# First blocks of an expert loop: overflow tables by counting, the residual's stores ahead of a gather, gates turned after unit 9, down biases in other PSUM banks

## The reference

```python
logits = hf @ w_router + b_router              # 32 experts, top 4 of each token
gates = softmax(top_vals)
# assignments sorted by expert, each expert padded to blocks of 128 rows
gu = xb @ w_gate_up[e] + b_gate_up[e]          # per block of 128 rows
gate, up = min(gu[:, :D], 7), clip(gu[:, D:], -7, 7)
act = (up + 1) * (gate * sigmoid(1.702 * gate))
y = act @ w_down[e] + b_down[e]
out = x2 + sum over the four experts of gate * y
```

## Time and profile before

| | before |
|---|---|
| median of 3 runs | 1726.53 us (1725.62 to 1729.35) |
| the profiled execution | 1726.46 us |
| its span, first to last instruction | 1724.6 us |
| PE busy | 1657.2 us (96% of the span) |
| DVE busy | 1351.2 us (78%) |
| ACT busy | 1094.6 us (63%) |
| POOL busy | 323.4 us (19%) |
| mean granted TensorE clock | 0.982 |
| bytes moved | 482.34 MB, mean 280 GB/s |

### The profile page before, as it was taken

The page is one execution under the profiler, slowest core; times in us unless marked ns, Lnnn a source line. Parts: engine busy times, 40 slices in busy tenths (PEclk is TensorE's granted clock), DMA queues, the critical chain, the costliest instruction groups (busy, mean ns, idle before and its releaser), DMA issues.

```text
span 1724.6 us, 23842 instructions
## 1 busy us (share of the span) xinstructions
PE 1657.2 (96%) x7974; PEld 1352.2 (78%) x7974; DVE 1351.2 (78%) x1089; ACT 1094.6 (63%) x989; POOL 323.4 (19%) x178
## 2 busy tenths in 40 slices
PE   7999999999987979999999999999999999999995
PEld 5797777888975758888888888888888888888884
DVE  4864555633546969999999999999999999999994
ACT  5323434322343657778777787778877788777873
POOL 0000000600004742122211321122211221112210
PEclk9999999999996989999999999999999999999998
DMA  8231222332535799999999999999999999999993
GB/s 269 74 97 51 73 74 74 92 122 74 180 146 186 266 322 364 377 364 376 381 385 372 361 381 382 380 373 365 382 379 377 373 365 388 380 373 364 377 387 82
DMA packets 211683, 482.34 MB, mean 280 GB/s; under 512 B 12539, under 2 KB 55075, under 8 KB 195123
## 3 DMA queue, kind: packets, MB, share of 16 engines
q1 hardware_dynamic: 201024, 453.99, 70.1%
q0 software_dynamic: 10624, 27.87, 7.9%
HBM read 469.05 MB, written 21.67 MB: 285 GB/s over the span
## 4 chain that ended last, share of the span: by engine, by line
PE 89%; POOL 3%; DVE 2%; issue 2%; DMA 2%; ACT 1%; SPq 0%; ACTq 0%; POOLq 0%; DVEq 0%
PE ps L575 27%; PE ps L577 27%; PE ps L576 27%; PE ps L755 2%; PE ps L761 2%; PE ps L779 2%; POOL slot_records L1487 1%; PE ps L689 1%; PE ps L678 1%; DMA out<-r 1%; PE ps L650 1%; DMA r<-in_x 1%; PE ps L669 0%; POOL work L1506 0%; PE ps L722 0%
## 5 line engine op out<-in xcount | busy, mean ns | idle before, releaser
L1236 DVE TENSOR_TENSOR zT<-raw,zT 128x2048 fp32r<-128x2048 f32 x96 | 221.4, 2307 | 70.4 <-ACT zT L988 67.1
L1236 DVE TENSOR_TENSOR w_lo<-more_raw,w_hi 128x2048 fp32r<-128x2048 f32 x96 | 218.0, 2298 | 15.9 <-ACT w_hi L988 15.8
L1236 DVE TENSOR_TENSOR zT<-more_raw,zT 128x2048 fp32r<-128x2048 f32 x96 | 220.0, 2291 | 4.0 <-ACT zT L988 4.0
L1236 DVE TENSOR_TENSOR w_lo<-raw,w_hi 128x2048 fp32r<-128x2048 f32 x96 | 217.3, 2290 | 0.0
L575 PE MATMUL ps<-w_hi,xT 128*128 128x512 f32 x512 | 216.3, 422 | 0.0
L575 PE MATMUL ps<-zT,xT 128*128 128x512 f32 x512 | 204.7, 400 | 10.9 <-DVE zT L1236 10.9
L988 ACT ACTIVATE zT<-more_raw 128x2048 fp32r<-128x2048 f32 x96 | 183.4, 1911 | 33.9 <-PE ps L577 33.9
L576 PE MATMUL ps<-zT,xT 128*128 128x512 f32 x512 | 201.2, 393 | 0.0
L577 PE MATMUL ps<-zT,xT 128*128 128x512 f32 x512 | 201.1, 393 | 0.0
L577 PE MATMUL ps<-w_hi,xT 128*128 128x512 f32 x512 | 201.0, 393 | 0.0
L576 PE MATMUL ps<-w_lo,xT 128*128 128x512 f32 x512 | 200.9, 392 | 0.0
(11 more groups left out here) (244 smaller groups left out, 3358.7 us busy)
## 6 DMA issues: line engine op xcount, KB each, us to landing
more_raw<-in_w_gate_up SPq DMA_DIRECT2D x129, 1024.0 KB, 6.0
raw<-in_w_gate_up SPq DMA_DIRECT2D x127, 1024.0 KB
raw<-in_w_down SPq DMA_DIRECT2D x65, 1024.0 KB
more_raw<-in_w_down SPq DMA_DIRECT2D x63, 1024.0 KB, 6.7
raw<-in_w_in SPq DMA_DIRECT2D x29, 1024.0 KB, 5.2
r<-in_x SPq DMA_DIRECT2D x8, 512.0 KB, 7.1
raw<-in_w_branch_conv SPq DMA_DIRECT2D x4, 1024.0 KB, 4.7
raw<-in_w_out SPq DMA_DIRECT2D x4, 1024.0 KB, 4.7
```

What stands on the lines that cost most here:

```text
L1236: nc.vector.tensor_tensor(expert_pair(1, c), chunk, expert_pair(0, c).bitcast(F32), ALU.subtract).then_inc(split_lo, 2)
```

## The change

- `over_experts` no longer makes two comparisons, a product and a product with the expert's number. It compares the overflow block's number with the running end `inc32` of each expert once, and sums the outcome: the count of experts that end before the block. One instruction on 15 columns adds 1 and caps at 32. The selectors and the block numbers follow in the same function.
- POOL's five stores of `x2` move ahead of `gather_next(1)` and of the tables.
- On PE, the gates' transpose moves from after unit 3 to after unit 9, `down_bias(0)` from after unit 7 to after unit 13, `down_bias(1)` from after unit 11 to after the turn of block 1's rows, and PE waits for the last addition before block 1. Both write banks 0, 1, 4 and 5 in place of 4 to 7, so `down_bias(0)` also waits for the first activation.
- On DVE, the split of chunk 3 moves ahead of `place_records`, the gates by expert to after split 4, copy and first activation to after split 6, the additions (now two instructions each) to after split 0 of block 1 and after the second activation, and split 1 of block 1 to the end.
- ACT waits for the additions at the head of each iteration.

```diff
--- before.py
+++ after.py
@@ -305,7 +305,6 @@
         byexp = work[:, 0:512].rearrange("p (b k e) -> p b k e", b=NB, k=TOPK)
         byoff = work[:, 512:1024].rearrange("p (b k e) -> p b k e", b=NB, k=TOPK)
         ov1 = work[:, 3072:3072 + MAXOVER * NE].rearrange("p (j e) -> p j e", e=NE)
-        ov2 = work[:, 3584:3584 + MAXOVER * NE].rearrange("p (j e) -> p j e", e=NE)
         xTh, xTl = xT[:, 0:KD], xT[:, KD:2 * KD]
         aT = oT[:, :, :, :].rearrange("p a b (c n) -> p (a b c) n", n=P)
         aTh, aTl = aT[:, 0:KD], aT[:, KD:2 * KD]
@@ -806,25 +805,25 @@
             def down_bias(n):
 
                 for b in range(NB):
-                    last = pe.matmul(ps[:, bk_D + b, :], gT[NE * b:NE * b + NE, :],
+                    last = pe.matmul(ps[:, bk_A + 4 * (b // 2) + b % 2, :], gT[NE * b:NE * b + NE, :],
                                      bdn[NE * b:NE * b + NE, 512 * n:512 * n + 512], start=True, stop=True)
                 last.then_inc(down_bias_pe, 1)
 
             for j in range(16):
                 gate_up(0, j)
-                if j == 3:
+                if j == 9:
                     pe.wait_ge(gates_ok, 1)
                     pe.transpose(ps[:, bk_D, 0:P], gmat.rearrange("p b e -> p (b e)"), ident).then_inc(gT_pe, 1)
-                if j == 7:
+                if j == 13:
                     pe.wait_ge(gT_ok, 1)
                     pe.wait_ge(down_bias_in, 16 * NB)
+                    pe.wait_ge(act_ok, 2)
                     down_bias(0)
-                if j == 11:
-                    pe.wait_ge(x2_biased, 1)
-                    down_bias(1)
-            pe.wait_ge(x2_biased, 2)
             next_rows(0, 0)
             next_rows(0, 1)
+            pe.wait_ge(x2_biased, 2)
+            down_bias(1)
+            pe.wait_ge(x2_biased, 4)
             with pe.Fori(1, nblk) as g:
                 pe.wait_ge(turned_read, tile(g, BEGIN))
                 for j in range(16):
@@ -1047,6 +1046,7 @@
             turned(0, ROWS1, xTh[:, 4:8, :], bk_T + 1)
             sigmoid(0, 1)
             with sc.Fori(1, nblk) as g:
+                sc.wait_ge(x2_biased, 4)
                 store_y(g, unit_base(g), g)
                 for c in range(2, CPE):
                     split_expert(g, c)
@@ -1359,6 +1359,7 @@
                                         xTh[:, 4 * half:4 * half + 4, :].bitcast(F32),
                                         ALU.subtract).then_inc(turned_read, 1)
             split_expert(0, 2)
+            split_expert(0, 3)
             place_records()
             gates()
             ve.wait_ge(blocks_ok, 2)
@@ -1392,28 +1393,27 @@
 
                 ve.wait_ge(down_bias_pe, n + 1)
                 cols = slice(512 * n, 512 * n + 512)
-                nc.vector.tensor_tensor(x2[:, :, cols], x2[:, :, cols], ps[:, bk_D:bk_D + NB, :],
-                                        ALU.add).then_inc(x2_biased, 1)
-
-            for c in range(3, 8):
+                for pair, bank in ((slice(0, 2), bk_A), (slice(2, 4), bk_D)):
+                    nc.vector.tensor_tensor(x2[:, pair, cols], x2[:, pair, cols], ps[:, bank:bank + 2, :],
+                                            ALU.add).then_inc(x2_biased, 1)
+
+            for c in range(4, 8):
                 split_expert(0, c)
-                if c == 3:
+                if c == 4:
                     gates_by_expert()
-                if c == 4:
+                if c == 6:
                     ve.wait_ge(gT_pe, 1)
                     nc.vector.tensor_copy(gT, ps[:, bk_D, 0:P]).then_inc(gT_ok, 1)
-                if c == 6:
-                    add_down_bias(0)
-                if c == 7:
                     clamp_up(0, 0)
                     activate(0, 0)
-                    add_down_bias(1)
             split_expert(1, 0)
-            split_expert(1, 1)
+            add_down_bias(0)
             turned(0, ROWS0, xTh[:, 0:4, :], xTl[:, 0:4, :], bk_T)
             turned(0, ROWS1, xTh[:, 4:8, :], xTl[:, 4:8, :], bk_T + 1)
             clamp_up(0, 1)
             activate(0, 1)
+            add_down_bias(1)
+            split_expert(1, 1)
             with ve.Fori(1, nblk) as g:
                 for c in range(2, CPE):
                     split_expert(g, c)
@@ -1493,8 +1493,6 @@
 
 
             jrow = cst[:, C_IOTA:C_IOTA + MAXOVER].unsqueeze(2).to_broadcast([P, MAXOVER, NE])
-            erow = cst[:, C_IOTA:C_IOTA + NE].unsqueeze(1).to_broadcast([P, MAXOVER, NE])
-            off_b = off32.unsqueeze(1).to_broadcast([P, MAXOVER, NE])
             inc_b = inc32.unsqueeze(1).to_broadcast([P, MAXOVER, NE])
             over = slice(NE, MAXBLK)
 
@@ -1508,22 +1506,15 @@
 
             def over_experts():
 
-                link(nc.gpsimd.tensor_tensor(ov1, jrow, off_b, ALU.subtract))
+                link(nc.gpsimd.tensor_tensor(ov1, jrow, inc_b, ALU.subtract))
                 link(nc.gpsimd.tensor_scalar(ov1, ov1, 0.5, None, ALU.is_gt))
-                link(nc.gpsimd.tensor_tensor(ov2, jrow, inc_b, ALU.subtract))
-                link(nc.gpsimd.tensor_scalar(ov2, ov2, 0.5, None, ALU.is_lt))
-                link(nc.gpsimd.tensor_tensor(ov1, ov1, ov2, ALU.mult))
-                link(nc.gpsimd.tensor_tensor(ov2, ov1, erow, ALU.mult))
+                link(nc.gpsimd.memset(eb[:, MAXBLK:NCOL], 1.0))
                 link(nc.gpsimd.tensor_copy(eb[:, 0:NE], cst[:, C_IOTA:C_IOTA + NE]))
-                link(nc.gpsimd.memset(eb[:, MAXBLK:NCOL], 1.0))
-                total(eb[:, over], ov2)
-
-            def over_selectors():
-
+                total(eb[:, over], ov1)
+                link(nc.gpsimd.tensor_scalar(eb[:, over], eb[:, over], 1.0, float(NE), ALU.add, ALU.min))
                 link(nc.gpsimd.tensor_scalar(sel[:, over, :], eb[0:3 * NE, over].unsqueeze(2).to_broadcast(
                     [3 * NE, MAXOVER, P]), cst[0:3 * NE, C_RMOD:C_RMOD + 1], None, ALU.is_equal))
-                link(nc.gpsimd.tensor_scalar(eb, eb, 1.0, -1.0, ALU.max, ALU.add))
-                nc.gpsimd.tensor_copy(ublk[:, 0:NCOL], eb).then_inc(over_ok, 1)
+                nc.gpsimd.tensor_scalar(ublk[:, 0:NCOL], eb, -1.0, None, ALU.add).then_inc(over_ok, 1)
                 gp.wait_ge(over_ok, 1)
 
             gp.wait_ge(blocks_ok, 2)
@@ -1555,14 +1546,13 @@
                 gp.wait_ge(y_out, 16 * blocks)
                 gp.sem_inc(rows_free, 1)
 
+            gp.wait_ge(x2_biased, 4)
+            for b in range(NB):
+                gp.dma_start(out_v[:, b, :], x2[:, b, :]).then_inc(out_set, 16)
+            gp.dma_start(out[S:S + P, :], x2[:, 0, :]).then_inc(out_set, 16)
             gp.wait_ge(slots_in, 16)
             gather_next(1)
             over_experts()
-            gp.wait_ge(x2_biased, 2)
-            for b in range(NB):
-                gp.dma_start(out_v[:, b, :], x2[:, b, :]).then_inc(out_set, 16)
-            gp.dma_start(out[S:S + P, :], x2[:, 0, :]).then_inc(out_set, 16)
-            over_selectors()
             gp.wait_ge(out_set, 16 * (NB + 1))
             with gp.Fori(1, but_one) as before:
                 g = before + 1
```

## The result

The changed kernel takes 1713.99 us in the median of 4 runs (1712.57 to 1715.58), the kernel before 1726.39 us (1725.62 to 1729.35; one run more than in the table of before). The ratio is 0.9925 with a 95% interval of 0.9908 to 0.9942: faster by 0.6 to 0.9%. The forecast was 1713.5. The profiled execution took 1712.57 us, with a span of 1710.7 against 1724.6, 13.9 us less.

The account below looks back on a forecast made before the run. PE is the bound, and POOL's chain decides when block 2 may go on. Gains of 4.1 - 0.3 + 13.3 - 5.2 + 1.0 = 12.9 us from 1726.46 us give 1713.5, range 1707.5 to 1720.5.

Parts of the forecast that it names:

- Block 0: Start of the kernel: PE resumes for block 1 at 568.5 instead of 572.64, 4.1 us earlier, with 0.3 charged for clock.
- POOL's chain: Records to uix copy, ahead of block 2: copy at 604.6, so block 2's whole 13.33 us excess goes.
- The 3.6 us in hand: Before block 2: margin between the uix copy at 604.6 and ACT wanting it at 608.2.
- What is late next is PE's own pace: Block 2: with the uix copy in time, PE's own work sets the time; block 2 takes about 35.6 us.
- 0.3 + 5.2 - 1.0: Block 1: 0.3 us restart clock, 5.2 lost to selectors holding DVE, 1.0 gained as four instructions that held DVE go.
- The gather ... cost 0: Block 2's rows, queued behind 2.62 MB of stores, land about 596, wanted at 598.3: cost 0, bounds 0 and 6 us.
- rival (B): POOL's queue is late after all, gather lands about 601, 3 us more wait with clock behind: about 1718; chance 0.2.
- The selectors: Block 1, about 597.5: selectors hold DVE 5.0 us, 1.5 covered, 3.5 PE wait plus 1.7 half clock: 5.2 us lost.
- (A): Selectors meet DVE's idle or PSUM work in block 1, so no loss: 1709.4; chance 0.2.
- (C): Stores and weights bunch on the DMA engines from 579 to 593, splits wait: 1720 to 1723; chance 0.08.
- (D): POOL's queue gets only what weights leave, gather lands at 634, 36 us late: slower, 1747; chance 0.05.
- (E): Some 8 of the tables' 11.4 us were waiting for DVE and stay; copy at 612, 4 us stall: about 1718; chance 0.05.

Follow-up runs that it names:

- POOL's part alone: Kernel before plus tables by counting, stores ahead of the gather and selectors in one go; PE, DVE and ACT in old order: 1711.21 us, ratio 0.9921.
- block 0's part alone: Changed kernel with POOL's part as before and a wait on all four additions ahead of the stores: 1726.4 us, ratio 1.0005.
- gather first: Changed kernel with gather_next(1) ahead of the five stores: 1712.81 us, ratio 0.9923.
- selectors twice: Changed kernel with the overflow selectors' instruction issued twice, same output: 1714.18 us, ratio 0.9945.
- selectors later: Changed kernel with overflow selectors, in five instructions, and block numbers made after block 2's scatter and gather; stores first: 1713.24 us, ratio 0.9935.
- selectors in five pieces: Changed kernel with the overflow selectors made in five instructions of 3 blocks each: 1714.9 us, ratio 0.9939.
- selectors later, wait on three: As selectors later, stores first, but PE waits for three of the four bias additions before block 1: 1711.66 us, ratio 0.992.
- no selectors: Changed kernel without the instruction that makes the overflow blocks' selectors: 1707.26 us, ratio 0.9908.
- gather first, no selectors: Changed kernel with the gather ahead of the stores and the overflow selectors left out: 1708.4 us, ratio 0.9902.
- selectors later, gather first: As selectors later, with the gather for block 2 ahead of the five stores: 1710.28 us, ratio 0.9916.

## Why the prediction was right, and where not

**Block 0, right in its stretch.** Block 1 was to begin 4.1 us earlier; the stretch is 3.96 us shorter. The wait ahead of it was put at 4.9 us and is 4.71. Unit 9 met its gates without a wait. The restart was charged 0.3; the first half of block 1 takes 14.26 us (568.80 to 583.06) instead of 13.97, 0.3 more. But the sum takes the 4.1 us as a gain by itself, and the runs do not bear that out. With POOL's part alone the distance is as short (111.76) as with both (112.82), and block 0's part alone gains nothing (127.56 against 125.27). By beginning block 1 earlier it also wants the gather's rows 3.3 us earlier, and that is where PE waits.

**POOL's chain, right in its outcome.** The uix copy was put at 604.6 and came at 608.59, 4.0 us later: the reading back of the records was issued at 580.53 in place of 578.3, 1.29 us passed ahead of the stores, and copy and gather took 1.92 and 2.90 us, where they had taken 0.18 and 1.07. The tables, 10.8 us in place of 13.5, won some of it back. The 3.6 us in hand were used up; block 1 had itself become longer, and so nothing waited. The 13.3 us went to 0.02. "What is late next is PE's own pace" held for block 2.

**Block 1, right in size, wrong in cause for the profiled execution.** The terms came to 0.3 + 5.2 - 1.0 = 4.5 us and the stretch is 4.82 us longer. But the step "The gather ... cost 0" failed. PE waited 2.97 us for it, with the clock at 0.50 behind it. Its latency was forecast well: an issue at about 582.9 (584.0 less the instruction's 1.07) and a landing at 596 are 13.1 us apart, and 13.1 were measured. The issue was 5.0 us late, at 587.87: some 2.2 from the reading back, 1.3 ahead of the stores, and 1.7 in the copy. Two us had been in hand, and 3.0 became PE's wait. The landing took 4.8 us after the issue in the kernel before, 12.2 to 16.0 us in the eight profiles with the stores ahead, and 6.3 to 10.7 in the three with the stores right behind it. This is the course of rival (B), which had been given 0.2.

**The selectors, right, and shown by removal.** The forecast had 3.5 us of wait and 1.7 of clock, 5.2 together; with the gather first the trace shows 3.39 and 1.7, and the removals say 4.0 to 5.1 us. Inside the 3.5, two terms were wrong and cancelled: the hold is 3.4 us and not 5.0, and none of it was covered where 1.5 had been taken. POOL's instruction takes 5.13 us, as reckoned from columns (5.0), but lets DVE go on sooner. As an estimate, the held instruction starts its own 0.69 us that long before it ends. In the kernel with the gather first that is at 601.29 + 4.06 - 0.69 = 604.66, 3.46 us after POOL's start at 601.20; with the selectors twice, at 601.06 + 4.08 - 0.69 = 604.45, 3.47 us after 600.98. The "0.5 us after POOL" in the front had two instructions in one row and could not show this.

**The two losses cover each other.** They fall in the same stretch, and PE pays for the later one. DVE of the changed kernel, with POOL's selectors at 601.66:

```profile
602.79 0.69 DVE L1388 TENSOR_TENSOR xT<-ps,xT 128x512 fp32r<-128x512 f32 x1 [2.31 <-ACT xT L1017]
603.40 0.68 DVE L1378 SCALAR_TENSOR_TENSOR work<-ps,work 128x512 f32<-128x512 f32 x1
604.17 1.65 DVE L1383 SCALAR_TENSOR_TENSOR work<-work 128x512 f32<-128x512 f32 x1
```

DVE itself had stood 2.31 us behind the gather, and then ran two instructions that read PSUM. L1383 came only at the end of the hold and lost 1.0 us (604.17 + 1.65 - 0.69 = 605.13, again 3.47 us after POOL's start). So the selectors cost PE next to nothing in this execution, and the gather cost it all: 3.0 us of wait and, with clocks of 0.50 from 601.0 to 604.0 and 0.57 from there to 607.5, another 3.0. Moving the selectors alone brings nothing while the gather is late (112.99). Removing the gather's lateness alone brings nothing in the distance (113.21), and as that profile is long and the changed kernel's short, at most some 2 us. Removing both brings 3.1 to 3.6 us (109.74, 109.19), again in long profiles, and so some 2 us more between like ones. The forecast charged one of them in full and the other with nothing. That the sum came out within 0.5 us of the median is luck in this part: the gather's price happened to be near the selectors'.

**What stays open.** The ten profiles of the new order in block 0, by when the records were read back (us after block 0 began), the landing of the gather after its issue, and PE's wait for its rows:

| profile | block 0 | read back | landing | wait |
|---|---|---|---|---|
| changed kernel | 33.1 | 44.8 | 13.1 | 2.97 |
| selectors later | 33.1 | 44.6 | 13.1 | 2.96 |
| selectors in five pieces | 33.1 | 44.3 | 12.2 | 2.09 |
| selectors later, wait on three | 33.2 | 46.4 | 13.7 | 3.62 |
| no selectors | 34.2 | 42.2 | 13.7 | 0 |
| selectors twice | 34.1 | 42.0 | 13.9 | 0 |
| gather first | 34.1 | 42.0 | 10.7 | 0 |
| gather first, no selectors | 34.1 | 41.9 | 6.3 | 0 |
| selectors later, gather first | 34.1 | 42.8 | 9.6 | 0 |
| block 0's part alone (gather first) | 33.1 | 44.4 | 8.4 | 0 |

In these profiles PE waits for the gather where the stores are ahead and the records are read back late; where only one of the two holds, it does not. The last row and the first are the one pair that differs in the gather's place and hardly in the reading back. Its weakness is that the stores come only 26 us behind that gather, not right behind it. The three other profiles with the gather first had their records early, so it is not shown that the version with the gather first has no wait with late records too.

The microsecond of block 0 is one of clock: in short profiles a matmul is down to 0.4 us some 3.0 to 3.7 us after block 0 begins, in long ones after 5.5 to 6.0 (granted clock 0.73 and 0.53 over the first 6 us, with the selectors later and with the gather first). The one with the wait on three gets there after 6.3 and is 33.2 us only because its wait ahead of block 1 is about 1 us shorter. What lets the clock rise early or late, and what delays the records, was not found.

**Rivals.** (A) fell with the removal of the selectors. (B) was what the profile of the changed kernel shows, with the time of the forecast. (C) is not seen: PE waits for no weights. (D) fell: the gather's rows landed at 601.0, not at 634. (E) fell: four instructions fewer shortened the tables, although the rest waits for DVE.

## What to carry to other kernels

When work is moved on one engine, look for what now runs beside it on the others: the same selectors cost 1.3 us in one place of a full block and 4 to 5 in another. A gain in one stage counts only if what the next stage waits for is ready too; the 4 us won in block 0 bought nothing until the selectors were gone. Two late things in one stretch hide each other, so remove them together before either is called free. And measure by the distance between fixed points of the timeline where a clock step elsewhere moves the span by as much as the effect, and see that the clock is alike between these points too.

## What was not expected of the hardware

A POOL `tensor_scalar` of 96 x 1920, float32 to bf16, held DVE instructions with two SBUF inputs for 3.46, 3.47 and 3.47 us of its 5.13, in three kernels. The Trainium skill, "SBUF — State Buffer", section Who interferes with whom, calls the contention for the shared ports an exclusive lock, names a DVE instruction with two SBUF inputs against a POOL instruction that reads SBUF as one case of it, and has the first to issue keep the ports for the whole instruction (this last where it speaks of the two-port modes). These runs agree that the other stands still, and that an instruction reading PSUM does not (L1388 and L1378 above, 0.69 and 0.68 us). On the length the measurement decides. The hold seems to work the other way too and costs POOL more: five pieces that do the same work took 12.01 us for 5.13.

The clock did not fall behind each wait of 2.0 us at the end of the loop: the same wait gave 14.4 to 14.5 us between the last two evictions in eight profiles and 12.8 to 12.9 in six.
